# First tap and bias of the short convolution on ScalarE, the other taps on VectorE

## The reference

```python
SSM_CONV = 4
...
def mamba2(z, xbc, dt_raw, conv_w, conv_b, dt_bias, a_log, d_skip, norm_w):
    b, s, _ = xbc.shape
    gn = SSM_NGROUPS * SSM_D_STATE
    xbc = lax.conv_general_dilated(xbc, conv_w[:, None, :], window_strides=(1,),
                                   padding=[(SSM_CONV - 1, 0)],
                                   dimension_numbers=('NWC', 'WIO', 'NWC'),
                                   feature_group_count=SSM_CONV_CH) + conv_b
    xbc = jax.nn.silu(xbc)
    xs = xbc[..., :SSM_D_INNER].reshape(b, s, SSM_HEADS, SSM_HEADDIM)
    bm = xbc[..., SSM_D_INNER:SSM_D_INNER + gn].reshape(b, s, SSM_NGROUPS, SSM_D_STATE)
    cm = xbc[..., SSM_D_INNER + gn:].reshape(b, s, SSM_NGROUPS, SSM_D_STATE)
```

## Time and profile before

| what | value |
|---|---|
| median of 3 runs | 2208.87 us |
| the profiled execution | 2205.2 us, of which the span 2202.7 |
| TensorE busy | 2077.7 us (94%) |
| VectorE busy | 1268.5 us (58%) |
| ScalarE busy | 992.9 us (45%) |
| GpSimd busy | 1283.4 us (58%) |
| mean granted clock | 0.972 of full speed |

### The profile page before, as it was taken

One profiled execution on the slowest core, in us unless ns is written; L12 is line 12 of the kernel. 1 busy time (PEld: TensorE's weight loads), 2 busy tenths in 40 slices (PEclk: granted clock), 3 DMA queues, 4 the chain that ended last, 5 costly groups with the idle time before them and its releaser, 6 DMA issues. The chain is left out here.

```text
span 2202.7 us, 46900 instructions
## 1 busy us (share of the span) xinstructions
PE 2077.7 (94%) x16820; PEld 2032.2 (92%) x16820; DVE 1268.5 (58%) x2869; ACT 992.9 (45%) x1449; POOL 1283.4 (58%) x624
## 2 busy tenths in 40 slices
PE   6888899999999999999879879999999999999997
PEld 6787899999999999999877869999999999999996
DVE  6754189538888444444375640994388884444443
ACT  4444454653333444444444444446533334444443
POOL 4344679976666455555353336798766665555552
PEclk8999899999999999999989989999999999999998
DMA  4422355554444555555344224545444435555552
GB/s 159 155 90 96 134 178 174 169 171 138 143 136 141 173 183 182 185 181 183 120 144 148 83 77 163 182 162 177 167 137 140 143 133 182 183 182 183 184 181 95
DMA packets 92817, 338.02 MB, mean 153 GB/s; under 512 B 10304, under 2 KB 10560, under 8 KB 92608
## 3 DMA queue, kind: packets, MB, share of 16 engines
q1 hardware_dynamic: 92736, 337.01, 45.3%
HBM read 335.92 MB, written 1.05 MB: 153 GB/s over the span
## 5 line engine op out<-in xcount | busy, mean ns | idle before, releaser
L448 POOL TENSOR_TENSOR WL<-ring,WH 128x1024 fp32r<-128x1024 f32 x360 | 909.6, 2532 | 504.6 <-ACT WH L1035 226.6
L1035 ACT CAST WH<-ring 128x1024 fp32r<-128x1024 f32 x512 | 536.5, 1048 | 856.4 <-PE PS L767 385.1
L472 POOL TENSOR_TENSOR HL<-G,HH 128x256 fp32r<-128x256 f32 x256 | 372.4, 1455 | 364.3 <-ACT HH L1128 364.1
L1582 DVE TENSOR_TENSOR WL<-ring,WH 128x1024 fp32r<-128x1024 f32 x248 | 303.9, 1225 | 410.5 <-ACT WH L1035 410.5
L766 PE MATMUL PS<-HH,WH 128*128 128x256 f32 x2048 | 512.5, 288 | 0.0
L829 PE MATMUL PS<-HH,WH 128*128 128x256 f32 x2048 | 502.6, 283 | 3.0 <-issue 3.0
L831 PE MATMUL PS<-HL,WH 128*128 128x256 f32 x2048 | 502.5, 283 | 0.0
L767 PE MATMUL PS<-HL,WH 128*128 128x256 f32 x2048 | 501.6, 283 | 0.0
L829 PEld LDWEIGHTS PS<-HH,WH 128*128 128x128 f32 x2048 | 393.2, 192 | 3.4 <-issue 3.4
L831 PEld LDWEIGHTS PS<-HL,WH 128*128 128x128 f32 x2048 | 393.2, 192 | 0.0
L767 PEld LDWEIGHTS PS<-HL,WH 128*128 128x128 f32 x2048 | 392.5, 192 | 0.0
(11 more groups left out here) (231 smaller groups left out, 2435.2 us busy)
## 6 DMA issues: line engine op xcount, KB each, us to landing
ring<-stream SPq DMA_DIRECT2D x636, 512.0 KB, 3.3
X<-x_t SPq DMA_DIRECT2D x4, 256.0 KB, 4.3
out_t<-H SPq DMA_DIRECT2D x1, 1024.0 KB, 3.9
CN<-consts SPq DMA_DIRECT2D x1, 907.5 KB, 7.8
PR<-params SPq DMA_DIRECT2D x2, 243.0 KB, 2.9
```

What stands on the lines that cost most here:

```text
L448: nc.gpsimd.tensor_tensor(WL[:, b, :], ring[:, slot, :], WH[:, b, :].bitcast(F32), ALU.subtract).then_inc(done, 1)
L472: nc.gpsimd.tensor_tensor(GL[:, s, :], G[:, tile, :], GH[:, s, :].bitcast(F32), ALU.subtract).then_inc(gl_ready, 1)
L1035: nc.scalar.copy(WH[:, b, :], ring[:, slot, :]).then_inc(hi_ready, 1)
L1582: V.tensor_tensor(WL[:, s % 2, :], ring[:, (U0 + s) % SLOTS, :], WH[:, s % 2, :].bitcast(F32), ALU.subtract).then_inc(vlo_ready, 1)
```

## The change

ScalarE makes the first tap and the bias: behind the eviction of each of the units 0 to 2 it waits for its own copy (`evac`) and runs two ACTIVATEs with the identity function, the scale from conv_w and the bias from conv_b, from XB into XC, and signals `conv_first` for each. VectorE waits for `conv_first` where it waited for `evac`, and makes the three other taps. The wait for `padded` goes from VectorE to ScalarE, ahead of the first `take`.

```diff
--- before.py
+++ after.py
@@ -205,6 +205,7 @@
         evac = sem("evac")
         padded = sem("padded")
         conv_ready = sem("conv_ready")
+        conv_first = sem("conv_first")
         conv_exp = sem("conv_exp")
         xc_ready = sem("xc_ready")
         roped = sem("roped")
@@ -922,8 +923,16 @@
                             upper(1)
                         act.wait_ge(h_ready, c + 1)
                         nc.scalar.copy(HH[:, c, :], H[:, c, :]).then_inc(hh_ready, 1)
-                    for n in (0, 1, 2, 3, 4):
+                    act.wait_ge(padded, 1)
+                    for n in range(N_XBC):
                         take(n)
+                        act.wait_ge(evac, n + 1)
+                        w = pr("conv_w").rearrange("p (b j) -> p b j", b=6)
+                        for b in (2 * n, 2 * n + 1):
+                            nc.scalar.activation(XC[:, b, :], XB[:, b, 0:SEQ], ACT.Identity, scale=w[:, b, 0:1],
+                                                 bias=pr("conv_b", b, b + 1)).then_inc(conv_first, 1)
+                    take(3)
+                    take(4)
                     act.wait_ge(conv_ready, 6)
                     nc.scalar.activation(CE[:, :, :], XC[:, :, :], ACT.Exp, scale=-1.0).then_inc(conv_exp, 1)
                     take(5)
@@ -1255,12 +1264,9 @@
                     norm(0, "norm_mix")
 
 
-                    dve.wait_ge(padded, 1)
                     for b in range(6):
-                        dve.wait_ge(evac, b // 2 + 1)
+                        dve.wait_ge(conv_first, b + 1)
                         w = pr("conv_w").rearrange("p (b j) -> p b j", b=6)
-                        step(V.tensor_scalar(XC[:, b, :], XB[:, b, 0:SEQ], w[:, b, 0:1], pr("conv_b", b, b + 1),
-                                             ALU.mult, ALU.add))
                         for j in range(1, CONV):
                             ins = V.scalar_tensor_tensor(out=XC[:, b, :], in0=XB[:, b, j:j + SEQ], scalar=w[:, b, j:j + 1],
                                                          in1=XC[:, b, :], op0=ALU.mult, op1=ALU.add)
```

## The result

The change made the kernel slower: the ratio of its time to the kernel before is 1.0021, 95% interval 1.0013 to 1.0029. The medians are 2213.5 us (22 runs) against 2208.0. The forecast was 2198.6 us, a gain of 10.3. The profiled execution took 2215.7 us for a span of 2213.6 and lies 2.2 us over its median.

The account below looks back on a forecast made before the run. The prediction took TensorE as the bound, with time to be had only from its 3.6 us wait for DUP and the low clock behind it. 2 x (2.75 + 2.4) = 10.3 us off 2208.87 gave 2198.6 us, range 2194.5 to 2206.5.

Parts of the forecast that it names:

- Six tensor_scalar leave VectorE: VectorE's convolution: nine operations held, six slipped through, three taps left; last ends at 60.7 us, gain 2.75 us a layer.
- From there to TensorE: TensorE's wait for VectorE's copies into DUP: 0.85 us in place of 3.6; 2.75 us a layer gained.
- The clock: Behind the DUP wait: clock stays high, transposes and project(6) take 6.9 us, not 9.31; 2.4 us a layer.
- Rival 1: Wait for DUP shrinks, but clock falls or gaps serve fewer taps: 2203.4 to 2206.5 us; chance 0.17.
- Six ACTIVATEs enter ScalarE: Behind ScalarE's first three evictions: two ACTIVATEs each, 0.5 us apiece, 1.0 a pair, at no cost.
- Does the gain hold further on?: At the attention scores: VectorE's score copies are late next, by 0.2 us, taken as 0.
- Rival 2: VectorE late at score copies or L622's blocks; only its own 2.75 us a layer remain: 2203.4 us; chance 0.12.
- Rival 3: ScalarE bounds the first pieces, its ACTIVATEs held and needing table loads: 9 us slower, 2218 us; chance 0.04.
- The sum: Whole kernel, two layers: 2 x (2.75 + 2.4) = 10.3 us gained, giving 2198.6 us; chance 0.64.

Follow-up runs that it names:

- e4: Kernel before, with only the six ACTIVATEs and their waits added on ScalarE, writing into unused space; VectorE still makes all taps: ratio 1.0000.
- e2: Changed kernel, with ScalarE's evictions of XS and T moved ahead of its casts of unit 11: ratio 0.9976 to the kernel before, median 2202.0 us.
- e5: Changed kernel with both moves, VectorE's of e1 and ScalarE's of e2: ratio 0.9970 to the kernel before.
- e9: e5 with ScalarE's Gelu of the compression also ahead of the casts of unit 11: ratio 0.9951 to the kernel before, median 2197.6 us.
- e1: Changed kernel, with VectorE's copy into DA and gate silu factor moved behind the first attention_scores: ratio 0.9966 to the kernel before, median 2200.1 us.
- e7: Kernel before, with the added reciprocal of e6, and the copy into DA and gate factor moved behind the first attention_scores: ratio 1.0007.
- e10: Kernel before, with the three moves of e9 but without the change itself: ratio 0.9998, median 2206.7 us.
- e8: Kernel before, with only ScalarE's move of e2 (evictions ahead of the casts of unit 11): ratio 1.0001.
- e6: Kernel before, with one more VectorE reciprocal of 336 elements (about 2.2 us) ahead of the copy into DA: ratio 1.0055.

## Why the prediction was wrong

- *Six tensor_scalar leave VectorE.* Right in the way of counting: nine are held as forecast, but four taps were left at the end and not three, and 60.8 us against 60.7 is that near only because the last subtraction was 0.3 us shorter. The busy time of 10.5 us that left VectorE moved the end of the convolution by 2.6. (By the prediction's own rows its gain is 63.43 - 60.73 = 2.70, not 2.75, and its bounds 1.1 and 3.7; that changes nothing here.)
- *From there to TensorE.* Right: the wait is 0.95 us, forecast 0.85.
- *The clock.* Right in this stretch: 7.2 us from the first transpose to L623, forecast 6.9. The reason was too bold. I took from one row that waits of 1.5 us in all leave the clock up, and e4 shows it falling behind waits of that size. Rival 1 named this, but it isn't what happened at the wait for DUP. What no rival had is that the fall can move: in six of the seven free layers of the changed kernel the clock is at 0.50 behind the scores instead, and 1.5 to 3.0 us a layer go there (e2, e5, e9, layer 1 of e1).
- *Six ACTIVATEs enter ScalarE.* The cost of nothing was right (e4). The size was not: 0.60 us each and 1.1 a pair, where I took 0.5 and 1.0; the Trainium skill's estimate of 0.59 ("ScalarE: Activation LUTs", What ACT_TABLE_LOAD costs) was the better one. Its rule to keep mul and add on VectorE (Rules for kernel authors) doesn't weigh a VectorE that is held by another engine, and this one is; the taps' 2.5 us show it.
- *Does the gain hold further on?* **This step failed.** I moved VectorE's operations by 2.75 us and TensorE's by 5.15, found the copies of the scores late next "with almost nothing to spare", and kept every duration as it was. But GpSimd's subtractions of unit 11 hang on the ring's pieces, which L622 sets free (ScalarE's cast ahead of them waits for the DMA in both kernels, 2.85 us before and 0.83 now), and so they moved with TensorE. They had been 0.8 us behind VectorE's last small operation; moved by about 4.5 us against about 2.6 for VectorE, they landed on it. L581 waits 4.65 us in place of 0.84, and with the 2.9 us more from there to L644 that is 6.7 us a layer against 4.8 won ahead of it. Not all of the 2.9 is the hold's: the free layers lose 1.5 to 3.0 there too. I had used exactly this effect for the taps and didn't look for it at the next place where GpSimd works. The trace of before had the row: the subtractions start at 89.18, less 5.15 is 84.0, and VectorE would be at small operations until 85.6. The Trainium skill ("SBUF — State Buffer", Who interferes with whom) says that a VectorE instruction with two SBUF inputs contends with a GpSimd instruction that reads SBUF, that one in a two-port mode contends with GpSimd too, and that whoever issues first has the shared ports for its whole instruction while the other is blocked. The trace agrees for the dt operations, the copy and the gate's addition, all from SBUF, and the copies of the scores out of PSUM took 0.95 us for the two with a subtraction running in e7. On the order of issue the starts in the traces are no sure guide below a tenth of a microsecond: two convolution operations of the kernel before that start 0.04 and 0.07 us ahead of a subtraction (at 41.73 and 47.45 us) took 2.73 and 2.62 us.
- *The rivals.* Rival 2 had the place right and the price wrong. It left VectorE's own gain standing (2203.4), because I thought of VectorE as late by tenths of a microsecond; held twice it was late by 4.65, and with the slower products behind that more went than had been won. Rival 3, the slower one, was about ScalarE and fell (e4). The range ended at 2206.5, since no likely case gave back more than was won; a hold costs GpSimd's whole instruction each time and isn't bounded by the gain.
- *The sum.* 10.3 us for the change where nothing is held is at the upper end of what the runs show: about 10 us by e9 against e10, 5.5 by e2 against e8, and 5 to 7 in the traces of these pairs. The near terms came out, 2.6 us a layer for the wait and 2.1 for the clock at DUP; the forecast failed further on, in the hold above all, and in part because the clock's term doesn't last past the scores.

## What to carry to other kernels

When a change makes one engine's stream earlier by more than another's, list the engines that hold each other up and check every place where they now overlap, not only the one that the change is about; a hold costs up to the whole length of the other's instruction, however small the held one is. Where VectorE's work must run beside long GpSimd instructions, put what reads PSUM there, and move small SBUF operations away. A gain that comes from the clock has to be followed further than the stretch where it arises, since the fall can come back at the next waits. And busy time that is mostly holding can't be taken off by removing operations: count how many are held and how many get through.

## What the runs showed of the hardware that was not expected

A VectorE operation of 128x4 elements, 0.17 us when free, took 2.30 us when it started 0.08 us behind a subtraction of GpSimd (e1), and an operation of 2.2 us put ahead of such a place in each layer cost 12 us over the two (e6). One copy that started 0.02 us behind a subtraction wasn't held, and there the subtraction took 2.85 us instead of some 2.35 (e6, layer 1). The granted clock fell to 0.50 behind waits of 0.9 and 0.6 us in e4 and stayed at 1.00 behind the same waits in the profiled execution of the kernel before, and in e2 it fell behind waits that left it at 1.00 in e8; a price for the clock that is read from one execution can be off by that.
